# A delta layer's head projections: one half-size product taken once for two pairs and split into seven quarter products

## The reference

```
hmod = rms_norm(x, norm_pre) * (1.0 + scale) + shift
qkv, z, b, a = split(hmod @ w_in)
q, k, v = split(silu(causal_dwconv(qkv)))       # four taps along time
o, s_new = gated_delta_rule(q, k, v, g, beta, s0)  # per head, in chunks
o = rms_norm(o, head_norm) * silu(z)
x = x + gate * rms_norm(o @ w_out, norm_post)
```

```
v_new = u_i - w_i @ state
state = state * exp(g_last) + k_dec.T @ v_new
```

## Time and profile before

| | |
|---|---|
| median of 3 runs | 1355.61 us (1355.04 to 1356.61) |
| profiled execution, span | 1354.8 us |
| TensorE busy | 1325.8 us (98%) |
| VectorE busy | 855.6 us (63%) |
| ScalarE, GpSimd busy | 434.6 us (32%), 331.1 us (24%) |
| one head of layer 1, heads 1 to 6 | 85.10 us |

### The profile page before, as it was taken

The page is one execution under the profiler, slowest core; times in us unless marked ns, Lnnn a source line. Parts: engine busy times, 40 slices in busy tenths (PEclk is TensorE's granted clock), DMA queues, the critical chain, the costliest instruction groups (busy, mean ns, idle before and its releaser), DMA issues.

```text
span 1354.8 us, 27409 instructions
## 1 busy us (share of the span) xinstructions
PE 1325.8 (98%) x11200; PEld 904.0 (67%) x11200; DVE 855.6 (63%) x1939; ACT 434.6 (32%) x1044; POOL 331.1 (24%) x450
## 2 busy tenths in 40 slices
PE   5999999999999999999999999999999999999997
PEld 3577776666654454667877788877788777875543
DVE  3847874355454375785886858858578586782246
ACT  3213443344431233521422414224143241432221
POOL 1023200010013232523312423224222242212352
PEclk9999999999999999999999999999999999999999
DMA  9531016002034522121212112121121211440124
GB/s 356 235 75 36 5 36 271 8 1 79 3 130 167 195 85 108 13 81 19 71 46 68 34 34 83 38 77 40 34 83 29 75 50 34 127 159 26 35 94 168
DMA packets 63297, 111.96 MB, mean 83 GB/s; under 512 B 34778, under 2 KB 38690, under 8 KB 61618
## 3 DMA queue, kind: packets, MB, share of 16 engines
q1 hardware_dynamic: 63172, 110.21, 24.2%
HBM read 91.79 MB, written 18.40 MB: 81 GB/s over the span
## 4 chain that ended last, share of the span: by engine, by line
PE 88%; DVE 7%; POOL 1%; DMA 1%; issue 1%; ACT 1%; SPq 0%; DVEq 0%; POOLq 0%; ACTq 0%
PE psum L1132 83%; PE psum L1135 5%; DVE mem L2963 1%; DVE mem L2774 1%; DVE mem L3288 1%; DMA mem<-x_dram 1%; DVE mem L3054 0%; DMA y<-mem 0%; DVE mem L3165 0%; DVE mem L2943 0%; DMA mem<-x 0%; POOL mem L954 0%; DVE mem L2780 0%; ACT mem L1915 0%; ACT mem L2087 0%
## 5 line engine op out<-in xcount | busy, mean ns | idle before, releaser
L1132 PE MATMUL psum<-mem 32*32 32x32 f32 (+12 forms) x10592 | 1264.1, 304 | 4.9 <-DVE mem L2475 1.5
L1132 PEld LDWEIGHTS psum<-mem 128*128 128x128 f32 (+4 forms) x10592 | 835.7, 143 | 401.7 <-issue 217.0
L2963 DVE SCALAR_TENSOR_TENSOR mem<-mem 128x576 f32<-128x576 f32 (+1 forms) x126 | 106.1, 842 | 0.0
L1135 PE MATMUL psum<-mem 128*128 128x128 f32 (+1 forms) x608 | 85.1, 278 | 17.2 <-ACT mem L1927 12.9
L1135 PEld LDWEIGHTS psum<-mem 128*128 128x128 f32 (+1 forms) x608 | 70.7, 144 | 41.4 <-issue 21.0
L2278 ACT ACTIVATE mem<-mem 128x128 f32<-128x128 f32 x72 | 22.0, 305 | 127.6 <-DVE mem L3213 74.4
L2164 ACT ACTIVATE mem<-psum 128x288 f32<-128x288 f32 x28 | 11.4, 407 | 104.0 <-PE psum L1132 104.0
L1011 POOL COPY mem<-mem 128x3 f32<-128x3 f32 x24 | 8.4, 348 | 148.9 <-DVE mem L2921 70.1
L2056 ACT ACTIVATE mem<-mem 128x256 f32<-128x256 f32 x72 | 35.5, 495 | 26.4 <-DVE mem L2697 26.4
L2744 DVE TENSOR_TENSOR mem<-mem,psum 128x512 f32<-128x512 f32 x28 | 19.1, 684 | 37.4 <-PE psum L1132 37.0
L2174 ACT ACTIVATE mem<-mem 128x576 f32<-128x576 f32 (+1 forms) x42 | 32.7, 779 | 28.0 <-DVE mem L2941 28.0
(11 more groups left out here) (260 smaller groups left out, 1277.2 us busy)
## 6 DMA issues: line engine op xcount, KB each, us to landing
mem<-modw SPq DMA_DIRECT2D x12, 2048.0 KB, 12.2
mem<-w SPq DMA_DIRECT2D x44, 512.0 KB, 4.3
mem<-x SPq DMA_DIRECT2D x10, 512.0 KB, 4.7
x_dram<-mem SPq DMA_DIRECT2D x9, 512.0 KB, 2.9
mem<-row_dram SPq DMA_DIRECT2D x8, 576.0 KB, 5.2
mem<-x_dram SPq DMA_DIRECT2D x9, 512.0 KB, 3.7
mem<-wout SPq DMA_DIRECT2D x1, 4096.0 KB, 15.0
mem<-gs SPq DMA_DIRECT2D x8, 512.0 KB, 3.6
```

The source lines that it names most:

```text
L1132: return pe.matmul(*a, **k)
L1135: return pe.transpose(out, in_, ident[0:n, 0:n])
L2963: x = dve.scalar_tensor_tensor(cvm, U1[:, m, lo + j:hi + j], CW[:, 3 * g + ORDER[m], j:j + 1], cvm, ALU.mult, ALU.add)
```

## The change

Product "4" of both pairs has the same moving operand, TD4. The new kernel takes this product once for both pairs (`BOTH`) and splits it by a second level of Strassen's method into seven quarter products `SUBS` of two calls each: 14 calls in place of 16. In `SLOTS` the slots 10 and 11 go from 3 calls each to 2 (the sum falls from 112 to 110). The order of the products becomes `PARTS`: 1, 6, 7, 5 of pair 0, the seven quarters, 2, 3 of pair 0, then 1, 6, 5, 7, 2, 3 of pair 1. The banks alternate by product, and each product waits until everything from two products back has been added or copied (`free_bank`).

VectorE gets five additions of quarters, two additions instead of one for the last products "7", and one addition `s21` of 576 columns with both inputs in SBUF, after (1, "6", 1); the additions of product "4" are gone. ScalarE copies two quarters more per head. GpSimd makes four weight sums of 128x256 per head (`both_sums`). In head 0 it makes TD4 before the copies into XW and YF, not after them, and then four differences of quarter tiles. Key taps move from slots 18 to 23 to slots 20 to 25, and the query taps to 26 to 31 (28 and 30 had none). The quarter tiles lie in the memory of layer 1's output gate, which SyncE writes to device memory (1 MB) before the layer and reads back in head 6. Also in head 6 the reloads of the gated rows wait for products 6, 5, 7 of pair 1 (closed in slots 30, 33, 35) where they waited for 6, 7, 5 (27, 30, 33), and the first half of the weight sums for a head's pair 0 waits for (1, "7"), now closed in slot 35 and before in slot 30.

The diff, cut to its core:

```diff
-SLOTS = ([3, 3, 3, 3, 3, 3, 3, 3] + [3] + [2, 3] + [3, 3]
+SLOTS = ([3, 3, 3, 3, 3, 3, 3, 3] + [3] + [2, 2] + [2, 3]
          + [2, 3] + [3, 2, 3] * 2 + [3, 3, 3] * 5
          + [3, 3, 2])
 TAIL = len(SLOTS) - 4
-HALVES = 2 * STEPS
-UNITS = HALVES * HALF
-PASSES = ("1", "6", "7", "5", "4", "2", "3")
-MADE = {"u2": (1, 2), "u3": (3, 4), "c22": (5, 7), "u4": (6, 8), "c21": (9, 10), "c11": (11, 12), "c12": (13, 14)}
-FREED = {"7": "u2", "5": "u3", "4": "u4", "2": "c21", "3": "c11"}
 KEY, QUERY, VALUE = 0, 1, 2
+BOTH = 2
+SUBS = ("1", "2", "6", "5", "7", "3", "4")
+PARTS = ([(0, s, j) for s in "1675" for j in range(2)] + [(BOTH, "4", s) for s in SUBS]
+         + [(0, s, j) for s in "23" for j in range(2)]
+         + [(1, s, j) for s in "165723" for j in range(2)])
+SIZE = [HALF // 2 if part[0] == BOTH else HALF for part in PARTS]
+UNIT = [(i, k) for i, n in enumerate(SIZE) for k in range(n)]
+UNITS = len(UNIT)
...
+PAIR_ADDS = {(0, "6"): ("u2",), (0, "7"): ("u3",), (0, "5"): ("c22", "u4"), (0, "2"): ("c11",), (0, "3"): ("c12",),
+             (1, "6"): ("u2",), (1, "5"): ("u4",), (1, "7"): ("c21", "c22"), (1, "2"): ("c11",), (1, "3"): ("c12",)}
+BOTH_ADDS = {"1": "a0", "2": "a0x", "6": "a1", "7": "b1", "3": "a1x"}
+ADDED = []
+for _q, _s, _at in PARTS:
+    if _q == BOTH:
+        ADDED += [(_q, _s, _at, BOTH_ADDS[sub]) for sub in _at if sub in BOTH_ADDS]
+        continue
+    ADDED += [(_q, _s, _at, _name) for _name in PAIR_ADDS.get((_q, _s), ())]
+    ADDED += [(_q, _s, _at, "s21")] * ((_q, _s, _at) == (1, "6", 1))
+COPIED = [part for part in PARTS if part[1] == "1" or (part[0] == BOTH and part[2] in ("5", "4"))]
...
+def half_bank(g, i):
+    return (len(PARTS) * (g - 1) + i) % 2
+def bank_left(g, i):
+    i -= 2
+    if i < 0:
+        g, i = g - 1, i + len(PARTS)
+    before = PARTS[:i + 1]
+    return (ADD0 + len(ADDED) * (g - 1) + sum(a[:3] in before for a in ADDED),
+            CP0 + len(COPIED) * (g - 1) + sum(part in before for part in COPIED))
...
-FIRST_TAP = {17: (KEY, 0), 20: (KEY, 1), 23: (QUERY, 0), 26: (QUERY, 1), 36: (VALUE, 0), 38: (VALUE, 1)}
-TAP = {18: (KEY, 0, 1), 19: (KEY, 0, 2), 20: (KEY, 0, 3), 21: (KEY, 1, 1), 22: (KEY, 1, 2), 23: (KEY, 1, 3),
-       24: (QUERY, 0, 1), 25: (QUERY, 0, 2), 26: (QUERY, 0, 3), 27: (QUERY, 1, 1), 29: (QUERY, 1, 2), 31: (QUERY, 1, 3),
+    return [(dh, i) for dh, i, k in units(p) if k == SIZE[i] - 1]
+CLOSES = {(dh,) + PARTS[i]: p for p in range(len(SLOTS)) for dh, i in closed(p)}
+FIRST_TAP = {19: (KEY, 0), 21: (KEY, 1), 25: (QUERY, 0), 27: (QUERY, 1), 36: (VALUE, 0), 38: (VALUE, 1)}
+TAP = {20: (KEY, 0, 1), 21: (KEY, 0, 2), 22: (KEY, 0, 3), 23: (KEY, 1, 1), 24: (KEY, 1, 2), 25: (KEY, 1, 3),
+       26: (QUERY, 0, 1), 27: (QUERY, 0, 2), 28: (QUERY, 0, 3), 29: (QUERY, 1, 1), 30: (QUERY, 1, 2), 31: (QUERY, 1, 3),
        36: (VALUE, 0, 1), 37: (VALUE, 0, 2), 38: (VALUE, 0, 3)}
...
             sp.wait_ge(sem("x1_out1"), 16 * (NT - HELD))
+            sp.dma_start(gate_dram, gate).then_inc(sem("x1_out1"), 16)
...
+                    if ahead == 1:
+                        sp.dma_start(gate, gate_dram).then_inc(sem("modb_in"), 16)
...
                 if h == H - 2:
                     sp.wait_ge(sem("row_kept"), 16 * (H - 2))
-                    for i, step in enumerate(("6", "7", "5")):
+                    for i, step in ((0, "6"), (2, "5"), (1, "7")):
...
-                    sp.wait_ge(sem("st_mm"), passed(h + 1, 1, "4"))
+                    sp.wait_ge(sem("st_mm"), passed(h + 1, 1, "7"))
...
+            def both_sums(g):
+                for m in (HEAD_M[0][1], HEAD_M[1][1]):
+                    wait(pool, sem(f"w1_in{m}"), 16 * g + 16)
+                if g == 1:
+                    wait(pool, sem("x1_out1"), 16 * (NT - HELD) + 16)
+                else:
+                    wait(pool, sem("st_mm"), passed(g - 1, BOTH, "4", "4"))
+                low, high = slice(0, HALF // 2), slice(HALF // 2, HALF)
+                pool.tensor_tensor(JS3, JA[:, low], JB[:, low], ALU.subtract).then_inc(sem("s_made"), 1)
+                pool.tensor_tensor(JS1, JB[:, low], JB[:, high], ALU.add).then_inc(sem("s_made"), 1)
+                wait(pool, sem("s_made"), weights_summed(g, BOTH, "s1"))
+                pool.tensor_tensor(JS2, JS1, JA[:, low], ALU.subtract).then_inc(sem("s_made"), 1)
+                wait(pool, sem("s_made"), weights_summed(g, BOTH, "s2"))
+                pool.tensor_tensor(JS4, JA[:, high], JS2, ALU.subtract).then_inc(sem("s_made"), 1)
+            def quarter_diffs():
+                wait(pool, sem("x1_out1"), 16 * (NT - HELD) + 16)
+                wait(pool, sem("t_ready"), DIFF0 + DIFF["t4"])
+                pool.tensor_tensor(QT3, QX22, QX12, ALU.subtract).then_inc(sem("t_ready"), 1)
+                wait(pool, sem("t_ready"), DIFF0 + QUAD["t3"])
+                pool.tensor_tensor(QX12, QX12, QX11, ALU.subtract).then_inc(sem("t_ready"), 1)
+                wait(pool, sem("t_ready"), DIFF0 + QUAD["t1"])
+                pool.tensor_tensor(QT2, QX22, QX12, ALU.subtract).then_inc(sem("t_ready"), 1)
+                wait(pool, sem("t_ready"), DIFF0 + QUAD["t2"])
+                pool.tensor_tensor(QT4, QX21, QT2, ALU.subtract).then_inc(sem("t_ready"), 1)
+                wait(pool, sem("t_ready"), DIFF0 + QUAD["t4"])
...
+                    wait(pool, sem("s_made"), weights_summed(h + 1, 0, "s4"))
+                if h == 0:
+                    wait(pool, sem("pj_mm"), 12)
+                    wait(pool, sem("t_ready"), DIFF0 + DIFF["t2"])
+                    pool.tensor_tensor(TD4, halves(1, 0), TD2, ALU.subtract).then_inc(sem("t_ready"), 1)
+                    quarter_diffs()
                 wait(pool, sem("n_ev1"), 7 * h + 5)
                 pool.tensor_copy(XW[0:32, :, 0:32], XT0[0:32, 0:NT - 1])
                 pool.tensor_copy(XW[32:64, :, 32:64], XT0[32:64, 0:NT - 1]).then_inc(sem("diag_ready"), 1)
@@ -1040,11 +1127,8 @@
                     i = pool.tensor_copy(YF[r, :, r], YT0[r])
                 c.tell(i, sem("diag_ready"), 2 * h + 2)
                 c.sync()
-                if h == 0:
-                    wait(pool, sem("pj_mm"), 12)
-                    wait(pool, sem("t_ready"), DIFF0 + DIFF["t2"])
-                    pool.tensor_tensor(TD4, halves(1, 0), TD2, ALU.subtract).then_inc(sem("t_ready"), 1)
                 if ahead:
+                    both_sums(h + 1)
                     head_sums(h + 1, 1)
...
+            def free_bank(g, i):
+                if g == 1 and i < 2:
+                    pe.wait_ge(sem("z_ev"), 2 + i)
+                    return
+                adds, copies = bank_left(g, i)
+                pe.wait_ge(sem("st_add"), adds)
+                pe.wait_ge(sem("st_cp"), copies)
...
+            def both_product(g, i, k):
+                sub = PARTS[i][2]
+                if k == 0:
+                    free_bank(g, i)
+                    if sub == "1":
+                        pe.wait_ge(sem("t_ready"), DIFF0 + DIFF["t4"])
+                        for m in (HEAD_M[0][1], HEAD_M[1][1]):
+                            pe.wait_ge(sem(f"w1_in{m}"), 16 * g + 16)
+                    elif sub == "6":
+                        pe.wait_ge(sem("s_made"), weights_summed(g, BOTH, "s2"))
+                        pe.wait_ge(sem("t_ready"), DIFF0 + QUAD["t2"])
+                    elif sub == "3":
+                        pe.wait_ge(sem("s_made"), weights_summed(g, BOTH, "s4"))
+                    elif sub == "4":
+                        pe.wait_ge(sem("t_ready"), DIFF0 + QUAD["t4"])
+                w, x = {"1": (JA[:, k], QX11[:, k]), "2": (JA[:, HALF // 2 + k], QX21[:, k]),
+                        "6": (JS2[:, k], QT2[:, k]), "5": (JS1[:, k], QX12[:, k]), "7": (JS3[:, k], QT3[:, k]),
+                        "3": (JS4[:, k], QX22[:, k]), "4": (JB[:, HALF // 2 + k], QT4[:, k])}[sub]
+                x = mm(B(half_bank(g, i))[:, 0:SUB], w, x, start=(k == 0 and sub in "125"),
+                       stop=(k == HALF // 2 - 1), skip_group_check=True)
+                if k == HALF // 2 - 1:
+                    x.then_inc(sem("st_mm"), 1)
...
+            def second_pair(g, sub):
+                wait(act, sem("st_mm"), passed(g, BOTH, "4", sub))
+                wait(act, sem("s1_ready"), 3 * (g - 1) + VALUE + 1)
+                j = int(sub == "5")
+                bank = half_bank(g, PARTS.index((BOTH, "4", sub)))
+                act.activation(U1[:, VALUE, PRE + j * SUB:PRE + (j + 1) * SUB], B(bank)[:, 0:SUB], ACT.Copy
+                               ).then_inc(sem("st_cp"), 1)
...
+                    dve.tensor_tensor(UD[:, j], c11, p, ALU.add).then_inc(sem("st_add"), 1)
+                    if (q, j) == (1, 1):
+                        dve.wait_ge(sem("st_add"), summed(g, 1, "6", "u2"))
+                        dve.wait_ge(sem("st_cp"), evicted(g, BOTH, "4", "4"))
+                        v = U1[:, VALUE, PRE:PRE + LO]
```

(80 more changed lines are left out.)

133 lines of the change are left out of this document (60 added, 73 removed).

## The result

The changed kernel takes 1377.33 us (median of 5 runs, 1376.68 to 1379.44) against 1355.81 for the kernel before in the same comparison: ratio 1.0161, interval 1.015 to 1.0172. It is slower by 21.5 us. The forecast was slower, 1367.8 us, range 1358 to 1376; the time lies 1.3 us above the range.

What follows compares the result with a forecast made beforehand. TensorE, busy 98% of the span, was taken as the bound. The terms, -6.8 + 9.5 + 2.1 + 2.1 + 2.8 + 2.5 = +12.2 us, took the median from 1355.61 to 1367.8 us, range 1358 to 1376.

Steps and rivals of the forecast that it cites:

- The gain: TensorE, seven heads: 14 calls fewer at .487 us each save 6.8 us, .97 a head; bound 7.8.
- Chunk 6: TensorE waits 1.36 us a head for VN behind s21 and a query tap: 9.5 us, bounds 7.7 to 11.2.
- Chunk 4: Slot 23's addition now stands ahead of RR: .3 us a head, 2.1 in seven heads; bounds 0 and 2.8.
- The quarters: Slots 14 to 19: each addition has one quarter's time before its bank is wanted again, so no loss taken.
- the parking of the gate: Writing 1 MB ahead of the layer takes 5 to 6 us but costs nothing; bound .5.
- End of a head: GpSimd's late weight sums meet VectorE's front: .35 us in each of six heads, 2.1; bounds 0 and 1.28.
- The norms: End of a head: norms behind GpSimd's late sums come 4 to 5 us later; TensorE's transposes need them.
- Rival (d): GpSimd's late sums hold VectorE's front for their whole length, 1.28 us in six heads: +5.6, 1373.4 us; chance .10.
- Layer 0's row: L2584 took 1.35 us for columns taking .28 elsewhere, ending as GpSimd's L823 did; used for head 0.
- Head 0: Once: TD4 gets in ahead of VectorE's small silu; TensorE's transposes of the value wait 2.8 us; bounds 0 and 3.5.
- Head 6: Once: reloads waiting for slot 35 hold up SyncE's queue and the weight loads: 2.5 us lost; bounds 0 and 4.4.

Runs made afterwards that it cites:

- with the waits out: Changed kernel with state addition in chunk 5, two GpSimd sums early, TD4 behind the silu, last reloads behind the state's store, s21 and slot 23's addition later: 1346.77 us.
- the tap alone: Kernel before, with the query tap of slot 31 moved to slot 30, ahead of the sample state's addition and VN: 1360.95 us (1.0034).
- The run without the wait: Changed kernel with head 0's TD4 held until the value's silu is done, quarter differences behind the copies and quarter weight sums: 1374.64 us (1.0144).
- the run without it: Changed kernel with head 6's sample state store issued ahead of the last two row reloads, not behind them: 1374.14 us (1.0138).
- the run with the sums early: Changed kernel with GpSimd's three pair 0 weight sums rewritten: two need only product (1, 6), the third is taken in the next head: 1370.03 us (1.0107).

## Why the prediction was wrong, step by step

- **The gain, 6.8 us.** Right: with the waits out, a head is 1.05 us shorter, 7.4 for seven.
- **Chunk 6, 9.5 us.** Right in place, order and, by the listed waits, size: 10.0. The state addition in chunk 5 took 7.9 of it away, and the tap alone gave .61 for the .58 worked out.
- **Chunk 4, 2.1 us.** Right in place, 1.3 by the listed waits.
- **The quarters, nothing; the parking of the gate, nothing.** No wait of TensorE lies there.
- **End of a head, 2.1 us.** This step failed. It measured 6.4 + 5.1 - 2.0 = 9.5 us. The prediction had seen the meeting of the late sums with VectorE's front, and of TensorE's waits the one for the outputs; the one for c11 it had not. It took .35 a head because the one row at hand (1.70 against 1.28) showed GpSimd held up and because part of it "is covered". Neither held. VectorE was the one held, .46 us at L3191 and .95 at L3193, and the front is a chain of small dependent instructions right ahead of what TensorE wants. The kernel before with the sums moved, and nothing else, loses 1.47 us a head of 1.59 held: there is next to no cover. The norms, which the step also named, cost nothing that the rows show; the two additions cost .2, by subtraction. Of the 9.5 us by which the forecast was low, 7.4 lie in this step. Rival (d) described this mechanism and gave it one chance in ten; its 1.28 a head would have made 1373.4. Layer 0's row, a short VectorE instruction that ended with GpSimd's sum, was the nearer one, and the prediction itself used it for head 0. The trace agrees with the Trainium skill's rule of a lock for a whole instruction (SBUF — State Buffer, section Who interferes with whom): L3193, .17 long elsewhere, took 1.12 and ended with the sum.
- **Head 0, 2.8 us.** Right in cause and in the wait, 2.6, with 5.13 us for the silu, foretold as about 5. That the clock falls behind the wait was in no term: 1.7 us more. The run without the wait is 2.7 us shorter, which matches the 2.8 by luck, as it lost time to the clock elsewhere.
- **Head 6, 2.5 us.** Right in cause and a little small: 3.3 by the waits, 3.2 by the run without it.

With the measured waits the sum is -6.8 + 10.0 + 1.3 + 9.5 + 2.6 + 3.3 = 19.9, and the spans differ by 20.7. That the two lie so close is in part luck, as shares that the sum leaves out nearly cancel. As the long silu of head 0 begins, the changed kernel's trace is 1.8 us ahead (616.41 for 618.22): in the run before, the granted clock was .50 from 26.00 to 29.20 us, in layer 0. That is between runs and not of the change, as far as the rows tell. Then the clock behind head 0's wait costs 1.7 us. And each head loses some .2 us more than its listed waits make, 2.37 for -.97 + 1.43 + .19 + 1.02 + .77 - .30 = 2.14, which fits a listed wait's costing more than is listed. The medians differ by .8 us more than the spans. The .8 us that the text ahead of the result puts between a run's time and its span isn't that of one run: in every run that has both on record they lie 1.7 to 2.3 us apart (1377.33 and 1375.5 for the changed kernel). The forecast doesn't hang on it.

## What to carry to other kernels

In a kernel like this one, which keeps its bound engine busy through an order written by hand, the slack of a step can be tenths of a microsecond (.18 at VN). A saving on the bound engine is worth what it says only after every helper that it moves has been placed again, and here that placement was worth over four times the saving. When a step on GpSimd moves, look at which VectorE instructions it will then stand beside: here a long one with SBUF inputs added most of its own length to a short instruction (4.85 us beside TD4, which takes 5.07 alone), and a chain of small dependent ones turned what was held into waits of TensorE almost whole (1.47 of 1.59). A queue that waits in order should have whatever is ready ahead of the instruction that waits.

## What the runs showed that was not expected

L3193, a TENSOR_SCALAR with one SBUF input and nine columns, was held for .95 us. The prediction had looked only for instructions with two SBUF inputs. The Trainium skill (SBUF — State Buffer, section Who interferes with whom) counts `tensor_scalar` among those that can take the shared pair of ports, under conditions on its operands; the trace agrees.

The clock after head 6's wait: in the run with the sums early TensorE waited 3.69 us for the output weight, and the granted clock, full before, was .52 for the next 5.85 us (nearly all of it at 1.2 GHz, the lower of its two levels; full is 2.4), then full again. The windows:

```profile
1218.98:1222.75 3.77, 0.08 (x9) 0.03 (x1) 2.05 (x5) 0.91 (x2) 0.00 (x0) 0.84 0.46 186
1222.75:1228.60 5.85, 5.85 (x13) 3.52 (x14) 0.36 (x1) 0.00 (x0) 0.00 (x0) 0.52 0.01 3
1228.60:1240.00 11.40, 11.40 (x273) 7.06 (x271) 5.85 (x11) 1.01 (x2) 1.22 (x4) 1.00 0.00 1
```

The 172 matmul instructions from 1222.75 took 11.50 us, and 8.74 in the changed kernel's own profile, where the wait was 3.3 us and the clock stayed at 1.00 behind it. In the run with TD4 behind the silu the wait was 3.11 us and the clock fell (.64 over 4.80 us). Head 0's wait for the silu shows the same: 2.56 or 2.57 us in five traces, with a stretch at half speed behind it in the changed kernel and in the runs with the state addition in chunk 5, the sums early and the last reloads late, and none in the kernel before with TD4 moved. So the length of the wait alone does not decide it here; what does is left open. A wait can thus cost over half its length again (1.7 us on 2.56), and one run differs from the next.
